# Branch gates in spare weight rows, part of a convolution on GpSimd, filler products and later loads in a one-core transformer kernel

## What is computed

```python
h = rms_norm(x, norm1_g)
proj = h @ w_in
(rx, rgate, q, kc, vc, ks, vs, kw, vw, nsa_g, mg_rnn, mg_attn) = jnp.split(proj, splits, axis=-1)
hr = rg_lru(causal_dwconv(rx, rnn_conv_w, rnn_conv_b), rg_w_a, rg_b_a, rg_w_x, rg_b_x, lru_lambda)
y_rnn = (hr * jax.nn.gelu(rgate)) @ w_rnn_out
```

```python
r = sigmoid(einsum('bsnc,ncd->bsnd', xb, w_a) + b_a)
i = sigmoid(einsum('bsnc,ncd->bsnd', xb, w_x) + b_x)
log_a = LRU_C * r * log_sigmoid(lam);  a = exp(log_a)
u = sqrt(-expm1(2.0 * log_a)) * (i * x)
h_t = a_t * h_{t-1} + u_t
```

## Time and profile before

| | us |
|---|---|
| median of 3 runs | 1151.5 (1149.93 to 1153.06) |
| the profiled execution | 1151.86 |
| its span, first to last instruction | 1150.1 |
| PE busy in the span | 1121.8 (98%) |
| DVE busy | 873.7 (76%) |
| ACT busy | 689.9 (60%) |
| POOL busy | 89.6 (8%) |
| weights and x read | 188.75 MB, 165 GB/s over the span |

### The profile page before, as it was taken

How to read it: one execution, slowest core, us unless ns; L and a number is a source line. 1 busy time by engine, 2 the same in 40 slices (tenths; PEclk the granted TensorE clock), 3 DMA queues, 4 the chain that set the end, 5 groups by cost and what they waited for, 6 DMA issues and landing times.

```text
span 1150.1 us, 25241 instructions
## 1 busy us (share of the span) xinstructions
PE 1121.8 (98%) x9449; PEld 1086.1 (94%) x9449; DVE 873.7 (76%) x1640; ACT 689.9 (60%) x1240; POOL 89.6 (8%) x141
## 2 busy tenths in 40 slices
PE   6999999999999999999999999999999999999997
PEld 6999999988999999999899999999998889999997
DVE  5789878687587998888777578767677867877774
ACT  6757864566646666555665466555565846655554
POOL 0000000055300000000023200000001330000000
PEclk9998999999999999999999999999999999999999
DMA  6675644722274776665544247766653424776661
GB/s 224 202 217 158 201 140 130 215 80 83 62 205 142 207 225 200 192 197 185 165 147 128 82 153 223 215 193 195 187 153 121 129 76 150 225 213 196 190 195 38
DMA packets 52925, 190.89 MB, mean 166 GB/s; under 512 B 6000, under 2 KB 6256, under 8 KB 52848
## 3 DMA queue, kind: packets, MB, share of 16 engines
q1 hardware_dynamic: 52416, 188.64, 54.1%
q10 hardware_dynamic: 432, 1.19, 0.3%
HBM read 188.75 MB, written 1.05 MB: 165 GB/s over the span
## 4 chain that ended last, share of the span: by engine, by line
PE 82%; DVE 7%; ACT 4%; DMA 3%; issue 2%; SPq 0%; DVEq 0%; ACTq 0%
PE bank L610 24%; PE bank L611 23%; PE bank L612 23%; DMA w_raw<-weight_stream 3%; DVE w_low L1776 3%; PE bank L729 2%; PE bank L741 2%; ACT w_high L1291 1%; DVE arena L2015 1%; PE bank L618 1%; PE bank L620 1%; PE bank L619 1%; PE bank L758 1%; DVE r_low L1800 1%; PE bank L756 1%
## 5 line engine op out<-in xcount | busy, mean ns | idle before, releaser
L1776 DVE TENSOR_TENSOR w_low<-w_raw,w_high 128x1024 fp32r<-128x1024 f32 x356 | 433.8, 1223 | 137.1 <-ACT w_high L1291 134.1
L1291 ACT ACTIVATE w_high<-w_raw 128x1024 fp32r<-128x1024 f32 x356 | 374.9, 1059 | 263.3 <-PE bank L612 163.6
L610 PE MATMUL bank<-h_high,w_high 128*128 128x256 f32 x1760 | 498.4, 283 | 11.9 <-DVE h_low L1814 10.3
L611 PE MATMUL bank<-h_low,w_high 128*128 128x256 f32 x1760 | 488.8, 278 | 0.0
L612 PE MATMUL bank<-h_high,w_low 128*128 128x256 f32 x1760 | 488.7, 278 | 0.0
L610 PEld LDWEIGHTS bank<-h_high,w_high 128*128 128x128 f32 x1760 | 332.4, 189 | 17.3 <-issue 11.9
L611 PEld LDWEIGHTS bank<-h_low,w_high 128*128 128x128 f32 x1760 | 332.6, 189 | 0.4
L612 PEld LDWEIGHTS bank<-h_high,w_low 128*128 128x128 f32 x1760 | 332.3, 189 | 0.0
L610 PE MATMUL bank<-r_high,w_high 128*128 128x256 f32 x942 | 267.6, 284 | 4.7 <-ACT arena L1703 2.6
L611 PE MATMUL bank<-r_low,w_high 128*128 128x256 f32 x942 | 262.2, 278 | 0.0
L612 PE MATMUL bank<-r_high,w_low 128*128 128x256 f32 x942 | 262.2, 278 | 0.0
(11 more groups left out here) (207 smaller groups left out, 1077.2 us busy)
## 6 DMA issues: line engine op xcount, KB each, us to landing
w_raw<-weight_stream SPq DMA_DIRECT2D x356, 512.0 KB, 4.1
x<-x_in SPq DMA_DIRECT2D x4, 256.0 KB, 6.2
small<-small_in ACTq DMA_DIRECT2D x1, 1001.5 KB, 9.1
out<-arena SPq DMA_DIRECT2D x3, 256.0 KB, 2.5
out<-arena SPq DMA_DIRECT2D x1, 128.0 KB, 2.7
out<-arena ACTq DMA_DIRECT2D x1, 128.0 KB, 2.9
small<-small_in ACTq DMA_DIRECT2D x1, 30.5 KB, 4.0
```

Source lines behind the costliest of these rows:

```text
L610: mm(out_ap, wh, high, start=start, stop=False, skip_group_check=True)
L611: mm(out_ap, wh, low, start=False, stop=False, skip_group_check=True)
L1291: fn(w_high[:, c % RING, :], w_raw[:, c % RAW, :], ACT.Copy).then_inc(high_ready, 1)
L1776: v.tensor_tensor(w_low[:, c % RING, :], w_raw[:, c % RAW, :], f(w_high[:, c % RING, :]), ALU.subtract).then_inc(low_ready, 1)
```

## The change

1. **Gates in spare rows.** The last tile of `rgate` and of `rx` has only 96 rows or fewer in use. The 48 gate columns are put in there, 24 in each, on rows 96 to 119. Stage `g` and its chunk go; `turn_branch_gates` turns the 32 rows of the two tiles with four transposes after lru group 5. There are 355 chunks; `lru` is now chunks 30 to 35.
2. **GpSimd.** The last tap (a product and an addition), the low part of the convolution, and the product of input gate and convolution are issued on GpSimd. VectorE's `scaled` of tile i waits for the last tap of tile i - 3 (`conv_ready`), which frees its buffer.
3. **Order.** In `w1` and `rx` both engines split one chunk later (`behind=1`); in `rx` ScalarE does the work of tile i first and then the split; the last rx tile's ScalarE work comes after lru group 2, the last two high parts of the convolution after groups 3 and 5. In `kvc` VectorE scales a tile before it splits.
4. **Start.** Nine products on a constant operand in bank 7 run first; a ScalarE instruction ahead of chunk 0 brings its table load forward; the 1 MB of constants is loaded after `w_high` of chunk 2; the squares come after those splits and the sums after the third kvc tile; the table of the square root is loaded before the sums, and `Exp` of the decay comes after them.

The core of the diff:

```diff
+            def last_tap(i):
+                pool.wait_ge(second_tap_ready, i + 1)
+                if i:
+                    pool.wait_ge(conv_ready, i)
+                nc.gpsimd.tensor_scalar(tap_product[:, 0:S - 3], rx_scaled[:, i % 3, 0:S - 3], par("rcw", i, 1), None,
+                                        ALU.mult).then_inc(tap_product_ready, 1)
+                pool.wait_ge(tap_product_ready, i + 1)
+                nc.gpsimd.tensor_tensor(conv[:, i, 3:S], conv[:, i, 3:S], tap_product[:, 0:S - 3],
+                                        ALU.add).then_inc(conv_ready, 1)
...
+            for i in range(RT):
+                last_tap(i)
+                if i:
+                    conv_low(i - 1)
+            conv_low(RT - 1)
...
+            pe.wait_ge(warm_ready, 1)
+            for _ in range(CLOCK_PRODUCTS):
+                mm(bank[7][:, 0:S], clock_operand[:, 0:P], clock_operand, start=True, stop=True)
...
-                         after=lambda i: norm_sums(0) if i == 1 else None)
+                         after=lambda i: norm_sums(0) if i == 2 else None)
...
-            stage("w1", hidden_cmp)
+            stage("w1", hidden_cmp, behind=1)
...
-            stage_behind("rx", rx_and_table)
-            conv_high(RT - 2)
+            for i in range(RT - 1):
                 rx(i)
+                split_high(BASE["rx"] + i - 1 + RING)
+            fn(stats[:, 6:7], eps_col, ACT.Sigmoid)
...
-                if t == 1:
+                if t == 2:
+                    rx(RT - 1)
+                    split_high(BASE["rx"] + RT - 2 + RING)
+                    split_high(BASE["rx"] + RT - 1 + RING)
+                if t == 3:
+                    conv_high(RT - 2)
+                if t == 5:
                     conv_high(RT - 1)
+                if t == 6:
                     branch_gates()
...
             def rx_scale(i):
+                if i >= 3:
+                    dve.wait_ge(conv_ready, i - 2)
                 scaled(rx_scaled[:, i % 3, :], "rx", i)
                 if i:
                     conv_tap(i - 1, 2)
...
-            stage("rx", rx_scale, then=rx)
+            stage("rx", rx_scale, then=rx, behind=1, first=0)
```

## The result

| | before | changed |
|---|---|---|
| median of 4 runs each, us | 1152.28 (1149.93 to 1153.79) | 1165.69 (1163.91 to 1170.88) |
| ratio, 95% interval | | 1.0127 (1.0095 to 1.0158) |
| span of the profiled execution | 1150.1 | 1168.9 |
| PE busy | 1121.8 | 1130.8 |

The change costs 13.4 us. The forecast was 1161.2, which is 9.7 us above the 1151.5 then known for before, with a range up to 1165.5; the median lies 0.2 us outside it. The profiled execution of the changed kernel is its slowest (1170.88), and so holds some 5 us that its median doesn't.

The account below looks back on a forecast made before the run. The prediction took TensorE, busy 98% of the span, as the bound, with VectorE setting the pace of rx. Lru ending 9.7 us later, earlier gains included, on a median of 1151.5 gave 1161.2; range 1159 to 1165, outer bounds 1154.5 to 1165.5.

Parts of the forecast that it names:

- the ring: In rx, ScalarE's split and VectorE's `scaled` wait for each other: 3.89 us a tile against 2.99 before.
- GpSimd's share: In rx, `w_low` waits 0.69 us for GpSimd's work, making 4.55 us a tile for tiles 3 to 8.
- Group 10: In lru, the bank of this group comes free at 124.2 us, after tile 10's convolution and one sigmoid.
- the end of lru: Stage lru ends at 132.0 us against 122.29 before, +9.7, gains ahead of it included.
- The start: Early table load and filler products bring the first w1 product forward: -1.1 us, bounds 0 to 3.
- The addition: In rx, GpSimd's two-input addition of the last tap takes 0.8 us, between 0.55 and 1.08.
- The gate products: Eleven on GpSimd beside lru's groups, 0.8 us each, hidden ahead of VectorE's first `lru_step`, at worst +1 us.
- Later stages read nothing new: Behind lru only the gate product is new, so the loss of 9.7 us there is the whole difference.
- rival B: In rx the ring doesn't bind: -11.3 us, 1140.2 in all; chance 0.08.
- stage g goes with its clock: Removing the stage between rx and lru saves its 7.3 us, and 3.4 us of half clock in lru.
- Rival A: In rx the ring alone counts, GpSimd's additions cost nothing: lru ends +5.3 us, 1156.8 in all; chance 0.22.
- Rival C: At the start the fillers don't raise the clock: +2.3 us, 1163.5 in all; inside the forecast's chance of 0.55.

Follow-up runs that it names:

- e2_vector: The changed kernel with all its new GpSimd work (last tap, convolution low part, gate product) back on VectorE, ScalarE's order kept: 1163.16 us, ratio 1.0088.
- a4_after: The changed kernel run again, unchanged, for a third profile, on the third chip: 1165.61 us, ratio 1.0129.
- a2_after: The changed kernel run again, unchanged, for a second profile, on the second chip: 1171.52 us in one run.
- e4_nofill: e3_both without the nine filler products on the constant operand at the start: 1149.72 us, ratio 0.998.
- e6_dummy_g: e3_both plus 48 unread products of 48 columns between rx and lru, as many as stage g had: 1151.78 us, ratio 0.9996.
- e3_both: The changed kernel with its new GpSimd work back on VectorE and ScalarE's weight split again ahead of the tile's work in rx: 1150.37 us, ratio 0.9996.
- e1_order: The changed kernel with only ScalarE's order in rx put back (weight split first), GpSimd's work kept: 1160.33 us, ratio 1.0069.
- e5: e3_both with low parts of tiles 2 to 7 behind tile 10's scaling and `w_low` 35 ahead of the last: 1150.79 us; on another chip 1146.79.

## Why the prediction was right and wrong

**Right: the ring.** Forecast 3.89 us by itself, measured 3.88; forecast 4.55 with GpSimd, measured 4.42 to 4.44 from tile 3 to 6 and 4.63 from 6 to 9; from tile 9 to 10, with the compression's work, 5.27 and 5.28. GpSimd's share was right in sum and not in its step: the forecast had `w_low` start 0.69 late behind the low part in every tile. In tiles 3 to 5 the low part begins 0.16 behind the start of `w_low` instead, and it is the second tap that is held (0.54 over e2_vector's 3.88). Only in tiles 6 to 8 is it `w_low`, by 0.2 to 0.5, and there the small copies that the forecast took for hidden show (4.14 to 4.41 in e2_vector). 6 x 4.55 = 27.3 was forecast from tile 3 to 9 and 27.2 measured: luck in part. Group 10 was forecast at 124.2 and came at 124.02, the end of lru at 132.0 and 132.09. Here two more errors cancelled: the first `scaled` came at 69.51, not 71.4, since w1 started at 56.87 and not 58.3, and tile 10 at 114.22, not 115.7; then GpSimd's product for tile 10 took 2.88 us beside two `w_low`, and its convolution was ready at 123.15 (forecast 123.3).

**The start** was mis-sized: -1.1 forecast, and 59.43 - 56.87 = 2.6 against the first profile of before. Against the second, where w1 starts at 57.43, it is 0.6: the start of before differs by 2 us from one execution to the next, which one profile can't show. The same holds for the end of lru, 122.29 in one and 120.16 in the other. So the +9.8 there would have been 11.9 with the other profile at hand; TensorE's waits in the k stage bring the two within 0.6 by 140 us.

**GpSimd.** The addition was forecast at 0.8 and took 0.63, the low part 0.74 alone; the product was put at 0.55 by the nearest line and took 0.93 with nothing beside it. Together 2.30 instead of 2.15. The gate products, put at 0.8 each, took 12.79 us for eleven from the first start to the last end, and end at 137.6, ahead of VectorE's first `lru_step` at 140.43, which waits for ScalarE: no wait of its own, but three `w_low` take 1.48 to 1.82 beside them. From the end of lru to 140 us the kernel loses 0.5, inside the "at worst +1".

**Wrong: the step from the front part to the total.** The text took whatever TensorE loses up to lru as the whole difference: "Later stages read nothing new". That held up to 300 us, where the three profiles of the changed kernel are 10.2 to 10.6 us behind, the forecast's 9.7 and under 1 us in the k stage. Behind that they lose 2.9 (a4_after) to 9.1 us (a2_after) more: 1.6 in products 0.1178 apart up to 357 us; 0.1 to 0.9 in a stall some 21 us behind the sums of the second norm, which neither profile of before has (nor have those of e4_nofill and e6_dummy_g); 6.4 in the net in two of the three profiles, and nothing in a4_after; and -0.1 to +1.0 behind it. a4_after, at 1165.16, is near the median, and of the 13.4 - 9.7 = 3.7 us that the forecast lacks it shows 0.8 up to 300 us and 2.9 behind. So the step that failed is the term behind the k stage, put at nothing: it measured 2.9 near the median and up to 9.1, with the net's 6.4 in some executions and not in others. How much of it the change brings about is open: the second profile of before has the 1.6 as well. Its range should have been in mine: the distance of 0.118 stood in the profile of before at the start of rx, where its second profile has 0.113. In w1 (48 products in 5.73 us) it does belong to the stage.

**Wrong: rival B's 1140.2.** That the ring doesn't bind was tried with e3_both and gave 1150.4. The step that failed is "stage g goes with its clock": 7.3 + 3.4 us were counted as if nothing waited behind them, though the text had just said that VectorE sets the pace of rx and that group 3 needs tile 10. With both removed, TensorE stood waiting for VectorE's `scaled` of tile 10 at 99.17, and behind the wait the clock fell to 0.50 all the same. The forecast itself went by VectorE's tile 10 and so was not hurt.

**Rival A** (ring alone, +5.3) was tried as e2_vector: +6.1 at the end of lru, but 1163.2 in all for its 1156.8. **Rival C** (fillers don't raise the clock) is ruled out: they do.

By the Trainium skill, GPSIMD Engine Reference, "Engine selection", elementwise work with two inputs belongs on VectorE. e1_order agrees as to the result: with that work on GpSimd a tile takes 3.48 us, without it 3.11. The estimate of 0.9 us from its table was too high for the operation itself, 0.63 to 0.74 here; what costs is the turn-taking.

## What to carry to other kernels

Before moving a step behind another on an engine, follow what its result feeds: if the engine that waits for it also makes the thing that the moved step now stands behind, the two form a ring, and its length is the sum over both engines however idle each looks: 3.88 us here, with ScalarE idle for 2.0 of them. Before counting a removed stage at its full length, look for who was late behind it; put a dummy of the same length back to measure its price. In this kernel, work moved to GpSimd beside a VectorE that reads two operands from SBUF was not taken off VectorE: count its time on both.

## What the runs showed of the hardware

TensorE's products of 256 columns start 0.1133 or 0.1178 us apart at the same granted clock of 1.00, and keep to one of the two for up to 188 us. In the first net of this kernel it makes 6.4 us. The same program had either of them there in different executions. The median of one kernel (e5) was 1150.79 in ten runs on one chip and 1146.79 in twelve on another, with before at 1152.4 and 1152.3 beside it: ten runs of such a kernel do not settle a difference of 3 us.

GpSimd and VectorE take turns: GpSimd's 0.93 us product took 1.89 and its 0.74 us low part 1.72 beside VectorE's two-input operations, which in turn grew from 0.47 to 0.95 and from 1.22 to 1.76, while VectorE's `scaled`, with one operand in PSUM, stayed at 0.41.
